# Two transformer blocks on one Trainium2 core: the residual multiplies folded into the norm, and the order of the attention's and mixer's side work changed

## The chip, the core and the metric

The kernel runs on one core of a Trainium2 chip. It is written out engine by engine: TensorE (PE), VectorE (DVE), ScalarE (ACT), GpSimd (POOL) and SyncE (SP) each have an instruction stream in program order, and semaphores join them. The metric is the device time of one execution in microseconds; the figure is the median of several executions.

## The reference

A first block works on 256 tokens of width 1024 (the latents), in fp32: a norm, 8 heads of dilated and 8 heads of block attention with relative bias, cross attention to 256 memory tokens, and a gated feed-forward with a causal convolution. A second part, of two layers, works on 512 tokens: those 256 latents and 256 context tokens (`ctx`), with conditioning vectors.

```python
def rmsnorm(x, g):           # first block
    y = xf * lax.rsqrt(jnp.mean(xf * xf, axis=-1, keepdims=True) + EPS)
    return y * g
    ...
        y = jnp.concatenate([rmsnorm(merge(ya, DIL_WIDTH), g_out_dil[l]),
                             rmsnorm(merge(yb, MOBA_WIDTH), g_out_moba[l])], axis=-1)
        h = h + y @ w_out[l]
        h = h + memory_cross_attention(rmsnorm(h, g_cross[l]), rmsnorm(mem, g_mem[l]), ...)
        h = h + conv_ffn(rmsnorm(h, g_ffn[l]), ...)
...
def modulate(x, shift, scale):
    return x * (1.0 + scale) + shift

def post_norm(x, y):         # second part: behind every mixer and feed-forward
    return layer_norm(ALPHA * x + y)
```

In the second part each of two layers is feed-forward, mixer, feed-forward. Each reads `modulate(x, shift, scale)` of the stream, multiplies its result by a gate, and `post_norm` gives the new stream; ALPHA is 4 to the power 0.25. The shifts, scales and gates come from `silu(c)` by a weight matrix of 1024 to 9 x 1024 a layer ("ada"). The mixer of layer 0 ("even") joins a gated linear attention (GLA, 4 heads, decays that are running sums of log gates, in chunks) with a latent attention (MLA, 4 heads of rope and non-rope parts). The mixer of layer 1 ("odd") is neighbourhood attention with context keys.

## The kernel before

**Tiles and products.** The stream X lies in SBUF as eight tiles X[:, k, :] of 128 features by 512 tokens: columns `lat` hold the 256 latents, columns `con` the 256 context tokens, and before those come in, `con` is scratch (att1's output y). A dense product runs in three passes on fp32r: high parts by high weights (L526), low part of the activation by high weights (L527), high part by low weights (L528). A weight chunk is 8 k-tiles by 256 columns. One DMA on SP's queue brings it into WF (three buffers). ACT casts it to the high part WH in two halves (`act_half`, L1041), DVE subtracts for the low part of the first half (`dve_split`, L1545), POOL for that of the second (`pool_split`, L2174). WH and WL have two buffers each. `PLAN` lists the chunks in the order in which PE uses them, and `splits_at(i)` says which chunk is split while chunk i is used: always the next one. Two chunks that PE interleaves (`pe_pair`) are listed in SECOND. A chunk of 256 columns at 256 tokens is 48 matmuls.

**Engine programs.** `pe_program`, `act_program`, `dve_program` and `pool_program` walk through the same stages, each with the part of its engine. An engine that waits holds up all that stands behind it. PSUM banks are handed out in a ring (`Banks.take`): PE waits for the event that empties the oldest bank.

**Start.** `pe_stat` sums the squares of x; ACT takes the root of the mean (Ln, then Exp); DVE scales a tile, ACT casts its high part and DVE subtracts the low one; then come the chunks qa, ka and va (two each). WIDE[0], the first chunk, is split beside the squares. Between the highs of x's norm and the split of qa's second chunk, ACT does two Silu of c and c_ctx with their table (L1484, L1485) and loads the log table again (L1044). Behind ka, ACT squares the memory and POOL adds the six squares (L2181).

**First attention (att1).** 16 units of one head each go through scores, exp, turning and weighing at steps i, i+2 and i+4 (`pe_attention_pairs`, 19 steps, two units at a time). `work1` lists what else is done in step i: scaling of the memory tiles ("mem"), and the chunks qb, kb, vb (inputs of the last eight heads) and km, vm (memory's keys and values). `work1 = spread(work1, 10) + [[]]*6` puts them all into the steps up to 9. `act_y` and `dve_y` put a finished pair's output into X[:, k, con] and, from k = 4 on, norm the tile four before, over a scratch HT[13]. `pe_pieces` and `dve_pieces` are parts of the ada product for the first gates ("pieces"), and stand behind the y statistic. Then come wout (4 chunks, L1719 adds to X), the cross norm, qm (the first two chunks as a pair), cross attention, wo, and the ffn norm.

**First feed-forward (f0).** `pe_ffn` does 11 gate and up chunks and 8 down chunks a half. The first pair is followed by `pe_ada_turn(5)`, whose bank DVE empties at L1585.

**Transition of the second part.** A feed-forward or mixer ends in `act_collect`, `pe_means` and a norm. `dve_modulate` makes of each X tile a product with the root in TMP[k % 3] (L1783, named "mt"); ACT applies scale and shift (`act_modulate`) and casts, DVE subtracts. While the next stage's chunks run, POOL multiplies each X tile by SQ, which is ALPHA times the root (L2187, `pool_residual`), so that X holds ALPHA times the normed stream, to which `dve_gated` adds gate times product. Into the first feed-forward of the second part (f10) no norm leads: POOL multiplies latents (L2341) and ACT context tiles (in `act_f0`) by ALPHA.

**Mixer of layer 0.** `pe_even`, `act_even`, `dve_even` and `pool_even` walk through e_q, e_lr, e_k, e_c (two chunks), e_v (two), uqn, uqr, e_r (two), ukv, then MLA attention. `gla_items` are the pieces of the GLA (`level` 0 to 19, `gouts`, `gnorms`), taken one by one by `some(n)` at places written out by hand, and the last ones by `work3`, beside the attention. The gates (d, n) in the order (0,0), (1,0), (0,1), (1,1) go through exp, Ln (L1361), a subtraction, and a running sum along the 256 tokens (L2012, two scans each). In the order before, gk is evicted ahead of the Ln, all four gates are scanned behind the split of e_k, and `dve_decays(1)` stands behind the second one.

## Time and profile before

| | us |
|---|---|
| three executions | 2321.92, 2323.25, 2324.7 |
| median | 2323.25 |
| the profiled execution, own time | 2322.09 |
| its span in the profile | 2320.3 |
| busy in the span: PE | 2218.7 (96%) |
| DVE | 1420.0 (61%) |
| ACT | 976.4 (42%) |
| POOL | 755.2 (33%) |
| mean granted clock of PE | 0.985 |

The profiled execution is one of its own; 1.8 us of its time lie outside the span. PE is busy 96% and the other engines far less. Some idle and slow stretches are short and lie at known places, so the views by time tell more than the sums.

### The profile page before, as it was taken

What the parts mean: (1) busy time and instruction counts of PE and PEld (TensorE: products, weight loads), DVE (VectorE), ACT (ScalarE), POOL (GpSimd) and SP (SyncE); (2) the same over time, 40 slices, a digit from 0 to 9 for tenths busy, and PEclk for the clock granted to TensorE, in tenths of its full rate; (3) what the DMA queues carried; (4) which work ended last, traced back from release to release, by engine and by line L of the source; (5) the groups of instructions that cost most, each with busy time, mean ns of one, the idle gap of its engine ahead of it and who ended that gap; (6) DMA issues with size and microseconds to landing.
All of it is one profiled execution on the core that took longest, in us unless ns stands there. A gap on an engine that the chain in (4) does not pass through costs nothing.

```text
span 2320.3 us, 34014 instructions
## 1 busy us (share of the span) xinstructions
PE 2218.7 (96%) x13148; PEld 1906.8 (82%) x13148; DVE 1420.0 (61%) x2103; ACT 976.4 (42%) x1585; POOL 755.2 (33%) x378
## 2 busy tenths in 40 slices
PE   6989989999999998988999999999999999989997
PEld 6978889998888876866788888878888878878997
DVE  3644454548887667757777766579756474447335
ACT  4655446543222336455442222253223254455443
POOL 3424325452222233521233322234222224214543
PEclk9999999999999999999999999999999999999999
DMA  7426535455464331120334443234454362214553
GB/s 256 171 95 263 224 128 191 159 178 198 165 227 168 132 118 51 53 73 1 127 109 150 168 172 119 99 136 152 169 205 158 104 147 92 73 55 140 177 180 105
DMA packets 79406, 329.98 MB, mean 142 GB/s; under 512 B 18912, under 2 KB 29280, under 8 KB 55696
## 3 DMA queue, kind: packets, MB, share of 16 engines
q1 hardware_dynamic: 79248, 327.81, 40.6%
q8 instruction: 107, 1.75, 0.3%
q14 instruction: 51, 0.42, 0.1%
HBM read 326.70 MB, written 1.08 MB: 141 GB/s over the span
## 4 chain that ended last, share of the span: by engine, by line
PE 82%; DVE 7%; issue 5%; ACT 5%; DMA 1%; POOL 0%; DVEq 0%; SPq 0%; ACTq 0%; POOLq 0%
PE ps L526 26%; PE ps L528 25%; PE ps L527 25%; PE ps L711 1%; ACT WH L1041 1%; PE ps L742 1%; DMA WF<-in_w 1%; PE ps L702 1%; DVE TMP L1621 1%; DVE WL L1545 1%; PE ps L687 1%; PE ps L721 1%; DVE AR L1958 0%; DVE TMP L1648 0%; DVE TMP L1560 0%
## 5 line engine op out<-in xcount | busy, mean ns | idle before, releaser
L2174 POOL TENSOR_TENSOR WL<-WF,WH 128x1024 fp32r<-128x1024 f32 (+2 forms) x253 | 598.0, 2364 | 1342.3 <-ACT WH L1041 1341.7
L526 PE MATMUL ps<-Hh,WH 128*128 128x256 f32 (+1 forms) x2536 | 860.3, 339 | 33.9 <-DVE WL L1545 10.8
L527 PE MATMUL ps<-Hl,WH 128*128 128x256 f32 (+1 forms) x2536 | 854.9, 337 | 0.0
L528 PE MATMUL ps<-Hh,WL 128*128 128x256 f32 (+1 forms) x2536 | 854.6, 337 | 0.0
L1041 ACT CAST WH<-WF 128x1024 fp32r<-128x1024 f32 (+3 forms) x507 | 466.3, 957 | 304.8 <-PE ps L528 296.6
L526 PEld LDWEIGHTS ps<-Hh,WH 128*128 128x128 f32 x2536 | 484.8, 191 | 98.9 <-issue 45.6
L528 PEld LDWEIGHTS ps<-Hh,WL 128*128 128x128 f32 x2536 | 484.8, 191 | 49.6
L527 PEld LDWEIGHTS ps<-Hl,WH 128*128 128x128 f32 x2536 | 485.1, 191 | 49.1 <-issue 0.2
L1621 DVE CUSTOM_DVE_ANT_0 TMP<-AR 128x1024 f32<-128x1024 f32 x216 | 416.0, 1965 | 8.6 <-DMA AR<-in_ada 7.3
L1545 DVE TENSOR_TENSOR WL<-WF,WH 128x1024 fp32r<-128x1024 f32 (+2 forms) x254 | 312.8, 1232 | 136.8 <-ACT WH L1041 136.3
L526 PE MATMUL ps<-HIDh,WH 128*128 128x512 f32 (+1 forms) x880 | 307.7, 350 | 3.8 <-DVE WL L1545 3.8
L527 PE MATMUL ps<-HIDl,WH 128*128 128x512 f32 (+1 forms) x880 | 305.7, 347 | 0.0
L528 PE MATMUL ps<-HIDh,WL 128*128 128x512 f32 (+1 forms) x880 | 305.7, 347 | 0.0
L1275 ACT ACTIVATE TMP<-ps 128x512 f32<-128x512 f32 (+1 forms) x88 | 47.8, 543 | 393.4 <-PE ps L528 393.4
L526 PEld LDWEIGHTS ps<-HIDh,WH 128*128 128x128 f32 x880 | 167.3, 190 | 26.6 <-issue 6.3
L527 PEld LDWEIGHTS ps<-HIDl,WH 128*128 128x128 f32 x880 | 167.4, 190 | 21.2 <-issue 0.7
L528 PEld LDWEIGHTS ps<-HIDh,WL 128*128 128x128 f32 x880 | 167.4, 190 | 20.7
L1860 DVE TENSOR_TENSOR TMP<-TMP,ps 128x512 f32<-128x512 f32 (+1 forms) x88 | 54.5, 619 | 184.2 <-PE ps L528 111.6
L1827 DVE SCALAR_TENSOR_TENSOR X<-ps,MOD,X 128x256 f32<-128x256 f32 x136 | 60.3, 479 | 132.9 <-PE ps L528 132.9
L1279 ACT CAST HIDh<-TMP 128x512 fp32r<-128x512 f32 (+1 forms) x88 | 49.9, 567 | 141.5 <-DVE TMP L1860 141.5
L526 PE MATMUL ps<-WH,Hh 128*128 128x256 f32 x320 | 91.9, 287 | 3.5 <-POOL WL L2174 3.5
L1862 DVE TENSOR_TENSOR HIDl<-TMP,HIDh 128x512 fp32r<-128x512 f32 (+1 forms) x88 | 58.6, 666 | 55.7 <-ACT HIDh L1279 55.7
(226 smaller groups left out, 2089.2 us busy)
## 6 DMA issues: line engine op xcount, KB each, us to landing
WF<-in_w SPq DMA_DIRECT2D x170, 1024.0 KB, 4.8
AR<-in_ada SPq DMA_DIRECT2D x120, 512.0 KB, 5.7
WF<-in_w SPq DMA_DIRECT2D x80, 704.0 KB, 4.1
AR<-in_piece SPq DMA_DIRECT2D x12, 1024.0 KB, 8.3
AR<-bias_rows SPq DMA_DIRECT2D x3, 1024.0 KB, 12.8
AR<-in_rpb SPq DMA_DIRECT2D x12, 256.0 KB, 6.6
AR<-in_cond SPq DMA_DIRECT2D x2, 1024.0 KB, 7.6
X<-in_x SPq DMA_DIRECT2D x2, 512.0 KB, 4.6
```

The source lines that it names most:

```text
L526: e.matmul(out, lh, rh, start=first, stop=False, skip_group_check=parts)
L527: e.matmul(out, lh, rl, start=False, stop=False, skip_group_check=parts)
L528: return e.matmul(out, ll, rh, start=False, stop=end, skip_group_check=parts)
L1041: e.copy(h[:, k0:k1, :], src[:, k0:k1, :]).then_inc(*up("w_hi", ("hi", i, q)))
L1275: e.activation(t[:, 0:T], ps[st, "g", n][:, 0:T], ACT.Silu).then_inc(*up("gate", (st, "ga", n)))
L1279: e.copy(HIDh[:, j, 0:T], t[:, 0:T]).then_inc(*up("hid_hi", (st, "hidh", n)))
L1545: e.tensor_tensor(l[:, k0:k1, :], src[:, k0:k1, :], h[:, k0:k1, :].bitcast(F32), ALU.subtract).then_inc(*up("w_lo", ("lo", i, 0)))
L1621: e.tensor_tensor_reduce(out=WIDE_TMP[r], in0=AW[x % 3], in1=COND[:, r, :], scale=1.0, scalar=0.0, op0=ALU.mult, op1=ALU.add, accum_out=MO ...
L1827: e.scalar_tensor_tensor(out=X[:, j, c], in0=ps[tile][:, c], scalar=MOD[:, l, 8 * g + j, r:r + 1], in1=X[:, j, c], op0=ALU.mult, op1=ALU.a ...
L1860: e.tensor_tensor(t, t, ps[st, "u", n][:, 0:T], ALU.mult).then_inc(*up("gated", (st, "m", n)))
L1862: e.tensor_tensor(HIDl[:, j, 0:T], t, HIDh[:, j, 0:T].bitcast(F32), ALU.subtract).then_inc(*up("hid_lo", (st, "hidl", n)))
L2174: e.tensor_tensor(l[:, k0:k1, :], src[:, k0:k1, :], h[:, k0:k1, :].bitcast(F32), ALU.subtract).then_inc(*up("p_lo", ("lo", i, 1)))
```

## The change

The residual multiplies go: gates are made as 1/ALPHA of what they were and the norm's epsilon as EPS/ALPHA^2, which leaves `layer_norm(x + y/ALPHA)` with the same value; DVE writes X times root back into X. In the first part, the order of work changes at the start, in att1, at the cross and ffn norms and in f0; in the mixer of layer 0 the order of Ln, scans, decays, evictions and the group norm changes.

```diff
@@ plan()
-    for c in range(4):
+    for c in range(3):
         out.append(("vm", k8, [("w_kv", rng(1024 + 256 * c, 256))]))
     wide("wout", "w_out", 1024)
+    out.append(("vm", k8, [("w_kv", rng(1024 + 256 * 3, 256))]))
...
-    work1 += [("km", i) for i in range(4)] + [("vm", i) for i in range(4)]
-    work1 = spread(work1, 10) + [[] for _ in range(6)]
+    work1 = [[] for _ in range(19)]
+    for i, items in ((0, [("mem", 0), ("qb", 0)]), (1, [("mem", 1), ("qb", 1)]), (2, [("mem", 2), ("kb", 0)]), (3, [("mem", 3), ("kb", 1)]),
+                     (4, [("vb", 0)]), (5, [("vb", 1)]), (6, [("km", 0)]), (8, [("km", 1)]), (10, [("km", 2)]), (12, [("km", 3)]),
+                     (14, [("vm", 0)]), (16, [("vm", 1)]), (18, [("vm", 2)])):
+        work1[i] = items
...
-    work3 = spread(gla_items[GLA_FIRST:], 16)
+    work3 = [[] for _ in range(19)]
+    for n, item in enumerate(gla_items[GLA_FIRST:]):
+        work3[min(2 * n, n + 6)] = [item]
@@ pe_attention_pairs: the pieces now ahead of the y statistic
-                    pe_stat(e, ("y", end // 4), S, [(HT[10], ("ysum", end // 4)), (HT[11 + end % 2], ("ysq", end))])
                     if end == 7:
                         pe_pieces(e, "y")
+                    pe_stat(e, ("y", end // 4), S, [(HT[10], ("ysum", end // 4)), (HT[11 + end % 2], ("ysq", end))])
@@ pe_ffn
-                pe_ada_turn(e, 5)
...
+                if n == 2:
+                    pe_ada_turn(e, 5)
@@ pe_program: idle matmuls ("load" on zeros, then on X), vm(3) ahead of qm, qm no longer a pair
+        pe_idle(e, "load", 7, zeros[:, 0:P], zeros, ("zeros",))
         pe_stat(e, "x", S, [(HT[0], ("xsum", 7))])
+        pe_idle(e, "x", 5, ident, X[:, 0, lat])
...
-        pe_pair(e, ac, *[(CH["qm"][c], S, [(("qm", j), [("qm", j)]) for j in (2 * c, 2 * c + 1)]) for c in range(2)])
-        for c in range(2, 4):
+        pe_work1(e, "vm", 3)
+        for c in range(4):
@@ act_y, dve_y: the y norm in place, cast and low one step later
-            dve_scaled(e, HT[13], X[:, k - 4, con], vec("g_out", k - 4), STAT[0][:, 0:S], ("yt", k - 4), ("root", ("y", 0)),
-                       ("yl", k - 5) if k > 4 else ("ml", 7))
+            dve_scaled(e, X[:, k - 4, con], X[:, k - 4, con], vec("g_out", k - 4), STAT[0][:, 0:S], ("yt", k - 4), ("root", ("y", 0)))
@@ act_f0, pool_program: gone
-                    e.mul(X[:, n, con], X[:, n, con], ALPHA).then_inc(*up("ctx_x", ("cxx", n)))
...
-            e.tensor_scalar(X[:, k, lat], X[:, k, lat], ALPHA, None, ALU.mult).then_inc(*up("p_x", ("f10", "res", k)))
@@ act_norm of post_norm, dve_modulation
-        e.activation(r, t, ACT.Ln, bias=eps).then_inc(*up("ln", (st, "ln")))
+        e.activation(r, t, ACT.Ln, bias=cst("eps_post")).then_inc(*up("ln", (st, "ln")))
...
-        if g != 3:
-            e.tensor_scalar(m[:, 16:24, :], m[:, 16:24, :], 0.5, None, ALU.mult)
+        e.tensor_scalar(m[:, 16:24, :], m[:, 16:24, :], (1.0 if g == 3 else 0.5) / ALPHA, None, ALU.mult)
@@ dve_modulate
-                    e.tensor_tensor(t[:, 0:T], X[:, k, 0:T], root[:, 0:T], ALU.mult).then_inc(*up("scaled", (st, "mt", k, 0)))
+                    e.tensor_tensor(X[:, k, 0:T], X[:, k, 0:T], root[:, 0:T], ALU.mult).then_inc(*up("scaled", (st, "res", k)))
...
+        e.tensor_tensor(X[:, 0, 0:T], X[:, 0, 0:T], root[:, 0:T], ALU.mult).then_inc(*up("scaled", (st, "res", 0)))
@@ act_even: Ln ahead of the split of e_k's successor and of the gk evictions; QR's con copy and KN
-        for j in range(2):
-            e.wait_ge(*at(("qrrot", j)))
-            e.copy(QR[:, j, con], ps["qr", j][:, con]).then_inc(*up("a_evict", ("qrc", j)))
...
-        for j in (0, 2):
+        for j in range(4):
             act_evict(e, KN[:, j, :], ("kn", j)).then_inc(*up("a_evict", ("kn", j)))
@@ act_program: first chunk's second half no longer ACT's; Silu moved
-        act_split(e, WIDE[0])
+        act_half(e, WIDE[0], 0)
...
-        e.activation(SC[:, :, 0], vec("c", 0, 8), ACT.Silu)
...
+            if c == 0:
+                e.activation(SC[:, :, 0], vec("c", 0, 8), ACT.Silu)
+                e.activation(SC[:, :, 1], vec("c_ctx", 0, 8), ACT.Silu).then_inc(*up("silu", ("silu",)))
+                act_logs(e)
@@ dve_even: scans of (d, 0) behind e_k's split, decays behind e_c's first split, scans of (d, 1) in the loop of e_v
+            if n == 0:
+                scan(d, n)
+        dve_splits(e, CH["e_c"][0])
+        dve_decays(e, 1)
...
         for i in range(2):
             dve_splits(e, CH["e_v"][i])
             some(1)
+            scan(*GATES[2 + i])
...
-        for j in (1, 3):
-            dve_evict(e, KN[:, j, :], ("kn", j))
-        some(2)
+        some(1)
...
+        work = [work3[0], gi + work3[1]] + work3[2:]
+        dve_attention(e, "mla", units3, 192 ** -0.5, work, dve_gla, end)
@@ dve_program: low split of the first chunk's second half; the six adds of the memory squares
+        dve_split(e, WIDE[0], 1)
...
+        for k in range(1, 7):
+            e.tensor_tensor(HT[0], HT[0], HT[k], ALU.add).then_inc(*up("d_sum", ("msum", k)))
@@ pool_program: the high cast of the first chunk's second half
-        pool_split(e, WIDE[0])
+        e.tensor_scalar(parts_of(WIDE[0])[0][:, k0:k1, :], staged(WIDE[0])[:, k0:k1, :], 1.0, None, ALU.mult).then_inc(
+            *up("p_hi", ("hi", WIDE[0], 1)))
...
-        for k in range(1, 7):
-            pool_sum(e, HT[0], HT[k], ("msq", k), ("msum", k - 1) if k > 1 else ("msq", 0), ("msum", k))
```

`pool_residual` goes with all its calls, and so do the SQ product behind `act_modulate` and the waits for it. `splits_at` of the pair (qm 0, qm 1) becomes plain; the chunk split behind wo is still f0_gu[1], and its two high casts now stand behind the squares and behind highs 0 to 2 of the norm.

## Rows read from the trace of the kernel before

**Rows 1.** Page: busy time and instructions of PE in the whole span

```profile
PE 2218.7 (96%) x13148; PEld 1906.8 (82%) x13148; DVE 1420.0 (61%) x2103; ACT 976.4 (42%) x1585; POOL 755.2 (33%) x378
```

**Rows 2.** Windows: PE, PEld, DVE, ACT, POOL busy us (instructions), PE clock, DMA share, GB/s

```profile
25.40:32.65 7.25, 7.16 (x47) 7.19 (x48) 2.68 (x2) 1.80 (x3) 5.52 (x2) 0.76 0.51 164
61.10:153.30 92.20, 91.86 (x793) 89.17 (x794) 49.70 (x111) 52.30 (x111) 39.76 (x17) 1.00 0.44 151
153.30:190.20 36.90, 27.40 (x182) 18.80 (x180) 19.48 (x58) 25.91 (x62) 1.64 (x3) 0.72 0.47 188
302.40:321.20 18.80, 12.19 (x101) 11.81 (x99) 11.12 (x21) 11.35 (x19) 7.78 (x4) 0.97 0.46 154
321.20:335.20 14.00, 14.00 (x96) 14.00 (x97) 5.34 (x8) 3.33 (x6) 2.88 (x2) 0.79 0.26 96
924.10:931.50 7.40, 7.36 (x26) 5.71 (x26) 6.46 (x10) 1.06 (x1) 1.71 (x1) 0.75 0.45 158
```

**Rows 3.** Timeline of the start: start us, us, engine, operation, [idle before <-releaser]

```profile
9.93 1.99 ACT L1041 CAST WH<-WF 128x1024 fp32r<-128x1024 f32 x2 [1.79 <-DMA WF<-in_w]
...
11.00 1.23 DVE L1545 TENSOR_TENSOR WL<-WF,WH 128x1024 fp32r<-128x1024 f32 x1 [1.74 <-ACT WH L1041]
...
11.99 2.44 POOL L2174 TENSOR_TENSOR WL<-WF,WH 128x1024 fp32r<-128x1024 f32 x1 [11.57 <-ACT WH L1041]
...
14.05 1.05 DVE L1560 SCALAR_TENSOR_TENSOR TMP<-X,VEC,STAT 128x256 f32<-128x256 f32 x2 [1.82 <-ACT STAT L1064]
...
15.76 0.55 PE L526 MATMUL ps<-Hh,WH 128*128 128x256 f32 x1 [5.22 <-DVE Hl L1555]
...
23.04 1.99 ACT L1041 CAST WH<-WF 128x1024 fp32r<-128x1024 f32 x2
...
25.49 0.36 PE L526 MATMUL ps<-Hh,WH 128*128 128x256 f32 x1 [1.98 <-DVE WL L1545]
...
26.28 2.40 DVE L1545 TENSOR_TENSOR WL<-WF,WH 128x1024 fp32r<-128x1024 f32 x1 [0.60 <-ACT WH L1041]
```

**Rows 4.** Groups by line, POOL: busy us, mean ns | idle before

```profile
L2187 POOL TENSOR_TENSOR X<-X,SQ 128x512 f32<-128x512 f32 (+1 forms) x40 | 65.2, 1634 | 0.0
...
L2341 POOL TENSOR_SCALAR X<-X 128x256 f32<-128x256 f32 x8 | 7.8, 980 | 1.7 <-DVE Hl L1760 1.7
```

**Rows 5.** Timeline, end of va and first attention's first chunks

```profile
54.79 0.35 PE L526 MATMUL ps<-WH,Hh 128*128 128x256 f32 x1 [1.96 <-POOL WL L2174]
...
58.08 1.99 ACT L1041 CAST WH<-WF 128x1024 fp32r<-128x1024 f32 x2 [6.27 <-DMA WF<-in_w]
```

**Rows 6.** Timeline, tail of the first attention

```profile
161.77 1.55 PE L742 MATMUL ps<-TMP,AR 128*64 128x128 f32 x12
...
167.63 1.55 PE L742 MATMUL ps<-TMP,AR 128*64 128x128 f32 x12
...
183.66 0.88 DVE L1560 SCALAR_TENSOR_TENSOR TMP<-X,VEC,STAT 128x256 f32<-128x256 f32 x2 [3.09 <-ACT STAT L1064]
```

**Rows 7.** Timeline of PE, cross norm

```profile
214.04 0.36 PE L526 MATMUL ps<-Hh,WH 128*128 128x256 f32 x1 [1.67 <-DVE Hl L1555]
```

**Rows 8.** Timeline, first feed-forward

```profile
320.89 0.18 DVE L1585 TENSOR_REDUCE MOD<-ps 128x8 f32<-128x32 f32 x1
...
321.17 0.56 PE L526 MATMUL ps<-Hh,WH 128*128 128x256 f32 x1 [5.03 <-issue]
```

**Rows 9.** Timeline of PE, first chunks behind the mixer of layer 0

```profile
1200.02 0.47 PE L526 MATMUL ps<-Hh,WH 128*128 128x512 f32 x1 [0.73 <-DVE WL L1545]
```

**Rows 10.** Timeline of the mixer of layer 0, e_k to e_c

```profile
918.49 3.37 DVE L2012 TENSOR_TENSOR_SCAN AR<-CST,AR 128x256 f32<-128x256 f32 x2
...
921.78 2.21 DVE L1545 TENSOR_TENSOR WL<-WF,WH 128x1024 fp32r<-128x1024 f32 x1
...
924.14 0.77 PE L526 MATMUL ps<-Hh,WH 128*128 128x512 f32 x1 [7.33 <-DVE WL L1545]
```

**Rows 11.** Timeline of PE, inside the MLA attention

```profile
1099.53 0.68 PE L721 MATMUL ps<-TMP,HAl 128*128 128x128 f32 x4 [3.08 <-issue]
```

More of the change, by code:

```diff
@@ L73, in const_array @@
     put("eps", np.full((P, 1), EPS, np.float32))
+    put("eps_post", np.full((P, 1), EPS / ALPHA ** 2, np.float32))
     put("one", np.ones((P, 1), np.float32))
@@ L1213, in act_collect @@
         after = [(st, "shifted", k) if k < 4 else (st, "x", k)]
-        if k == 0 and st + "res" in RESIDUALS:
-            after.append((st, "res", KT - 1))
         if k in (4, 5, 6):
@@ L1256, in act_modulate @@
                 e.copy(Hh[:, k, 0:T], t[:, 0:T]).then_inc(*up("h_hi", (st + "h", k)))
-        e.mul(SQ[:, 0:T], STAT[0][:, 0:T], ALPHA).then_inc(*up("mean", (before, "up")))
     def act_cond(e, st):
@@ L1355, in act_even @@
             e.activation(TMP[i], TMP[i], ACT.Exp, scale=-1.0).then_inc(*up("decay", ("gexp", d, n)))
+        for i, (d, n) in enumerate(GATES):
+            e.wait_ge(*at(("gexp", d, n)))
+            e.activation(TMP[i], TMP[i], ACT.Ln, bias=one).then_inc(*up("decay", ("gln", d, n)))
         act_splits(e, CH["e_k"][0])
@@ L1358, in act_even @@
             act_evict(e, GK[:, j, :], ("gk", j)).then_inc(*up("a_evict", ("gk", j)))
-        for i, (d, n) in enumerate(GATES):
-            e.wait_ge(*at(("gexp", d, n)))
-            e.activation(TMP[i], TMP[i], ACT.Ln, bias=one).then_inc(*up("decay", ("gln", d, n)))
         for j in range(2):
@@ L2203, in pool_swiglu @@
                 pool_splits(e, CH[st + "_gu"][n])
-                if before and n < KT:
-                    pool_residual(e, st, before, n, T)
             for n in range(KT):
```

159 lines of the change are left out of this document (78 added, 81 removed).

## The prediction, made before the kernel was run

> **What bounds the kernel now.** I read the page's busy times first, then the windows, then the timeline around each hole of the matmul engine. PE is busy 2218.7 us of a span of 2320.3 us [rows 1], so it is the bound, and only two things can be won without removing matmuls: the 101.6 us in which it idles, and the stretches in which its matmuls run at half pace after an idle. The chain of waits says the same, since nearly all of it lies on matmul lines. The windows show where both sit [rows 2]. From 61.1 to 153.3 us, where each pair of attention steps has weight chunks beside it, PE is busy 91.86 of 92.2 us at a granted clock of 1.00. From 153.3 to 190.2, where the chunks have run out, it is busy 27.40 of 36.9 at a mean of 0.72, so more than half of the time at the lower of its two levels (1.2 and 2.4 GHz). The same pattern, smaller, stands at 302.4 to 335.2 and at 924.1 to 931.5. The change adds idle matmuls and moves the rest, so I price it as idle time removed, plus pace won back, minus holes that appear.
>
> **Start.** PE's first product comes at 15.76, and its next hole ends at 25.49, where it waits for a low split [rows 3]. That split waits for ACT's high casts at 23.04, which stand behind the two Silu instructions and their two table loads. The change moves Silu and both tables into the first key chunk, which has slack. So the 1.98 us wait goes, and with it the slow stretch behind it: 25.4 to 32.65 has 7.16 us of matmul at a mean clock of 0.76 [rows 2], which at full clock is 7.16 x 0.76 = 5.4, so 1.7 less. Against it stands the cast of the second half of the first chunk, now on POOL, and its low split, now on DVE ahead of the norm. No row shows POOL casting such a tile. Its subtract of the same tile took 2.44 us [rows 3]; its own tensor_scalar on 256 columns took 0.98 [rows 4], so four of them are 3.9, which is the upper end, and DVE's pace on the tile, 1.23, is the lower. I take 2.4, the row of the same shape. From 9.9, when the tile is there and ACT casts it now, it ends at about 12.4. DVE's first split runs beside it; a DVE subtract beside a POOL one took 2.40, alone 1.23 [rows 3], so it ends at 13.4 and the second at 14.6, and the norm, which could begin at 14.05, begins some 0.7 later (0 to 2.2). Start: -2.0 -1.7 +0.7 = -3.0, range -1.5 to -4.5. The seven and five idle matmuls fill time in which PE waits anyhow (5.22 us before 15.76), cost nothing, and may bring the first chunk to full clock (a rival, below).
> That the two subtracts met is what the trace shows, and it speaks against a POOL cast in this place. The Trainium skill, SBUF — State Buffer, section "SBUF: two separate sides", goes further: a DVE operation with two SBUF inputs and a GpSimd operation share a port pair under an exclusive lock, and the first to start holds it for its whole instruction. By that rule DVE's split would start only behind the cast, at 12.4, and both end near 14.9, the norm 0.8 late. The page GPSIMD Engine Reference, section "Engine selection", says that one-input operations on GpSimd run at roughly line rate; by that the cast would be done near 11.2 and the norm not late at all, so the start would be -3.7. No row here shows a POOL cast of this size.
> The six adds of the memory norm move from POOL to DVE. The wait of 1.96 us at 54.79 for POOL's low split, which stood behind them, goes [rows 5], but the cast at 58.08 waited 6.27 us for its transfer, and that one isn't earlier by more than PE's slack behind it. I count -0.7, range 0 to -1.9.
>
> **First attention.** The items of work1 stood at steps 0 to 9; now they reach step 18, so the last pairs get a chunk each. In the old tail a pair of steps came every 5.86 us (161.77, 167.63) [rows 6] with little matmul in it. What PE did in 153.3 to 190.2 is 27.40 x 0.72 = 19.7 us of work at full clock [rows 2]. One value chunk (vm 3) leaves the stage: 48 matmuls of 0.12 us, 5.8. So 13.9 of work stands there, and the idle that can't be filled: the chain from the last statistic to the first scaled tile (the norm's first tile comes at 183.66, 3.09 after DVE's last work [rows 6]), 3.2 by itself. 13.9 + 3.2 = 17.1 against 36.9 would be -19.8. I take -18, since seven chunks can't fit ten gaps evenly, range -12 to -21. The y norm now done in place adds no instruction, only an order: high casts shift one step later, behind ACT evictions that have slack at 52.3 busy of 92.2 [rows 2].
> The chunk vm 3 comes back in front of the query chunks, beside the cross norm. There PE waited 1.67 us for the norm [rows 7]; of the 5.8 the hole swallows that: +4.1, range +3.5 to +5. The feed-forward norm's casts, moved: -0.3 (0 to -0.6).
>
> **First feed-forward.** PE is busy 12.19 of 18.8 us from 302.4 to 321.2, and 14.00 of 14.00 at 0.79 behind it [rows 2]. The hole of 5.03 us ends when DVE has reduced the bank of the ada turn (320.89, then the matmul at 321.17) [rows 8]. With the turn behind chunk 2 no chunk waits for that bank. Idle 6.6 + pace 14.0 x 0.21 = 2.9 makes 9.5; what stays is ACT's pace of casts, for which I leave three small holes of 2.6 in sum. So -6.8 (range -4 to -8.5). What is late next: ACT's high cast of the fourth chunk. The eight X*ALPHA of ACT and of POOL (0.98 us each [rows 4]) go; nobody waited for them.
>
> **The residual pass.** POOL's multiply by ALPHA times the root, 40 of them, 65.2 us [rows 4], has idle POOL around it, so removing it is worth nothing by itself. DVE now writes X times root into X where it wrote a temporary: same count, and one multiply more per transition, 0.7 us behind the low parts, under a chunk pair of some 22 us. What the pass did cost is the port: DVE slows beside POOL, and at the transition behind the mixer PE waited 0.73 for DVE's low split at 1200.02, which follows DVE products that ran beside POOL's multiplies [rows 9]. Four such transitions: -1.0, range 0 to -3. The factor ALPHA moves into the gates and the root's epsilon: nothing.
>
> **Mixer of layer 0.** The hole before 924.14 is 7.33 us, behind DVE: two scans (3.37), decays, then the low split of 2.21 [rows 10]. The next 7.4 us run at 0.75 [rows 2], so 1.8 more. Now the second pair of scans stands beside the value chunks, Ln of the gates ahead of ACT's evictions of gk, and the split of the first c chunk before the decays. So both go, and 0.2 of small ones: -9.3 (range -5 to -9.5). The scans then delay the c norm beside e_v by about 1.0; the level item moved off ACT's copies gives about 1.0 back. The KN evictions, all four on ACT now, and the group norm taken into attention step 1 lift part of the holes around the MLA attention (3.08 us at 1099.53 [rows 11]): -2, range 0 to -3. Mixer: -11.3.
>
> **Sum.** -3.0 -0.7 -18 +4.1 -0.3 -6.8 -1.0 -11.3 = -37.0. The profiled execution took 2322.1 us (span 2320.3 and 1.8 around it), 1.2 under the median of 2323.25; 2322.1 - 37.0 = 2285.1, and I say 2285.
>
> **Rivals.**
> 1. *The attention pairs are set by DVE and ACT, not by PE.* If a pair needs its old 5.86 us and the chunk beside it isn't overlapped (11.6 a pair against 8.56), six and a half pairs cost 20 us more: 2305. (8.56 is a chunk of 5.8 and a pair's matmuls, 2.8.) Against it: 91.86 of 92.2 us busy with DVE at 49.7 and ACT at 52.3 [rows 2]. Chance 0.12.
> 2. *Slower: the stage falls to the lower clock.* Where the chunks are spread thinly over steps 6 to 18, a hole per pair may keep PE at 1.2 GHz. The rows show it: the old tail ran at 0.72 with its holes, and the stretch behind the hole of 5.03 us at 0.79 [rows 2, 8]. The stage has some 58 us of PE work at full clock from step 6 on (seven chunks of 5.8, 13.9 of the tail, 4 of the pairs ahead); at half clock that is 58 more, so 2285 + 58 = 2343, slower by 21. It decides from 37 us of such work on, where the gain is used up; it needs in every pair a hole like the one at 25.49, behind which the clock fell. A chance of 0.04, since the one long stretch with chunks has 0.34 us of idle in all. The Trainium skill, TensorE: Matmul & The Clock Gate, "HAM oscillation", says that micro-idles of PE can make the clock swing between its levels; by that rule such a stage would be slow throughout.
> 3. *More is won.* The idle matmuls warm the first chunk (worth what it was worth behind 25.49, 1.7), the holes before the mixer's scores and in the first feed-forward close wholly, and the att1 tail reaches 19.8: 2285 - 9 = 2276. Chance 0.15.
> 4. *Holes only move.* The feed-forward waits one chunk later (+4), the mixer waits in the c norm (+5) as the scans are now ahead of it: 2294. Chance 0.10.
> 5. *The change doesn't do what it says:* the tail stays, since the spread chunks wait for their splits and PE idles ahead of them for as long as before: 2285 + 18 = 2303, and 2320 if the first feed-forward and the mixer keep their holes too (6.8 + 11.3). Chance 0.02.
>
> **How the numbers follow.** The forecast, 2285, has chance 0.57 with a range of its own of 2277 to 2293. The whole range runs from rival 3's lower side, 2272, to most of rival 1, 2302; it leaves out rivals 2 and 5 and the upper side of 1. About 0.2% of this kernel, 4.6 us, is what a measurement can tell from no change. Slower is rival 2 (0.04), same 0.02 for rival 5's far end and what lies between, the rest faster.
>
> **What the profile after should show.** Start: first product between 16 and 17, no hole near 25, clock 1.00 from then on. Att1: 153 to the first wout chunk at 1.00 with PE over 90% busy; y's norm at some 165 to 172. A value chunk ahead of the query chunks. F0: no hole over 2 us. Mixer: no hole over 2 us between the k and v chunks; DVE's second scans beside L526 of e_v. No POOL rows of L2187. POOL's busy time down by 65 to 80 us. PE idle falls from 101.6 to some 78: of the 37.0, 1.7 + 7.7 + 2.9 + 1.8 = 14.1 is pace and not idle. Wrong would be: clock under 0.9 in att1, or a PE wait for a scan or a c norm over 4 us.

## The result, and the profile after

The changed kernel takes 2297.09 us (median of 2292.81, 2294.47, 2299.71 and 2299.92) against 2323.47 beside it: a ratio of 0.9885, interval 0.9865 to 0.9905. That is 26.4 us less; the forecast was 38 less and 2285, and 2297 lies in the range of 2272 to 2302. The profiled execution is the one of 2299.92, the slowest of the four; its stages say more than its sum.

The page of the changed kernel: span, busy times, and the chain that ended last by engine.

```profile
span 2298.1 us, 33979 instructions
...
PE 2221.8 (97%) x13172; PEld 1911.5 (83%) x13172; DVE 1404.5 (61%) x2117; ACT 970.0 (42%) x1571; POOL 677.7 (29%) x324
...
PE 86%; DVE 6%; ACT 4%; issue 3%; DMA 1%; POOL 1%; DVEq 0%; SPq 0%; ACTq 0%; POOLq 0%
```

POOL's busy time fell by 77.5 us and the span by 22.2. PE is idle 76.3 us instead of 101.6, where some 78 was foretold. PE's busy time rose by 3.1 us, with the idle matmuls in it (1.2 to 6.8 us and 10.3 to 13.8, some 9 us), so the others lost about 6 of it; 14.1 of pace were to be won back. The holes that remain have slow stretches behind them too.

The account by stages is made from PE's first product of each stage, in the two profiled executions.

| stage | before | after | difference | foretold |
|---|---|---|---|---|
| start to the first chunk of att1 | 60.99 | 57.64 | -3.35 | -3.7 |
| att1, to wout | 123.15 | 108.12 | -15.03 | -18 |
| wout, vm 3, qm, to wo | 74.57 | 79.94 | +5.37 | +4.1 |
| cross attention's output, ffn norm, to f0 | 31.91 | 31.26 | -0.65 | -0.3 |
| f0 | 231.94 | 224.29 | -7.65 | -6.8 |
| f10 | 348.18 | 349.55 | +1.37 | 0 |
| mixer of layer 0 | 284.75 | 284.74 | -0.01 | -11.3 |
| all behind it, to the end of the span | 1164.80 | 1162.59 | -2.21 | -1.0 |
| sum | 2320.29 | 2298.13 | -22.16 | -37.0 |

The row of the mixer is the answer to most of the question: a price of 11.3 us was given, and the stage is as long as before. The changed kernel's 284.74 us are at the long end, though. Three edited kernels below with the very same mixer (f1_turn_old, s1_no_idle, s3_rows_late) take 282.5 us in their profiles, a fourth (a1_work1_old) 283.8; so the fair difference is about -2.2 us, still far from -11.3.

Windows of the changed kernel over the stages of [rows 2]: att1 in two parts, the first feed-forward's start, and the e_c chunks of the mixer.

```profile
57.60:124.60 67.00, 66.77 (x567) 63.96 (x567) 44.73 (x106) 40.89 (x95) 25.84 (x12) 0.95 0.42 146
124.60:165.70 41.10, 37.24 (x312) 32.72 (x309) 20.84 (x51) 27.91 (x65) 12.47 (x7) 0.96 0.55 198
276.90:307.00 30.10, 29.24 (x236) 28.54 (x237) 19.88 (x37) 17.42 (x28) 10.25 (x5) 1.00 0.37 121
896.60:904.00 7.40, 7.40 (x45) 5.94 (x44) 4.64 (x4) 3.03 (x4) 4.17 (x2) 1.00 0.20 53
```

The bare tail of att1 is gone: 37.24 of 41.1 us busy at 0.96, where [rows 2] had 27.40 of 36.9 at 0.72. The feed-forward has 0.86 us of idle in 30.1. From 896.6 to 904.0, where the hole of 7.33 us had ended, PE is busy all the time at full clock.

Timeline of the start: start, duration, engine, operation, idle time before it and its releaser.

```profile
9.64 2.77 POOL L2312 TENSOR_SCALAR WH<-WF 128x1024 fp32r<-128x1024 f32 x1 [9.21 <-DMA WF<-in_w]
...
10.66 1.23 DVE L1560 TENSOR_TENSOR WL<-WF,WH 128x1024 fp32r<-128x1024 f32 x1 [1.47 <-ACT WH L1048]
...
12.44 1.23 DVE L1560 TENSOR_TENSOR WL<-WF,WH 128x1024 fp32r<-128x1024 f32 x1 [0.56 <-POOL WH L2312]
...
15.10 0.36 PE L529 MATMUL ps<-Hh,WH 128*128 128x256 f32 x1 [1.35 <-DVE Hl L1570]
...
55.19 1.99 ACT L1048 CAST WH<-WF 128x1024 fp32r<-128x1024 f32 x2 [8.56 <-DMA WF<-in_w]
...
57.64 0.55 PE L529 MATMUL ps<-Hh,WH 128*128 128x256 f32 x1 [3.58 <-DVE WL L1560]
```

The first product comes at 15.10, not between 16 and 17. POOL's cast took 2.77 us, beyond my 2.4, and yet the norm starts at 13.58, ahead of the old 14.05 [rows 3]: ACT, free of the second cast, has the root 1.25 us earlier (12.77 against 14.02). The norm could have begun then, but stands behind DVE's second low split, which waits for POOL's cast. The last two rows show that from there on PE's gain is lent: the cast of the next chunk waits 8.56 us for its transfer (6.27 before [rows 5]), PE waits 3.58 us behind it, and a slow stretch follows.

Five waits of PE in att1, wout and the mixer of the changed kernel (1.65 and 1.5 us at 1022.00, 1003.24 and 1073.54 are of the same order as the smaller ones).

```profile
138.14 0.96 PE L705 MATMUL ps<-AR 64*128 64x128 f32 x12 [2.58 <-DVE TMP L1653]
...
169.25 0.36 PE L529 MATMUL ps<-Hh,WH 128*128 128x256 f32 x1 [1.00 <-DVE Hl L1570]
...
934.11 1.16 PE L877 MATMUL ps<-AR 64*128 64x128 f32 x15 [1.42 <-POOL AR L2251]
...
966.96 1.35 PE L885 MATMUL ps<-AR 64*128 64x256 f32 x10 [3.03 <-DVE AR L1953]
...
1015.14 1.05 PE L877 MATMUL ps<-AR 64*128 64x128 f32 x14 [2.87 <-POOL AR L2251]
```

None of the five was in the forecast by place. The fourth and fifth are inside the mixer and are what the runs below take apart.

### The profile page after: what moved, and what is told of

Read it like the earlier page. It is cut to its first block, busy times and chain, and to the rows that moved or that the text cites. A ratio compares the mean times of both kernels' runs of the same rounds, so it can differ in the third digit from the quotient of the medians.

```text
span 2298.1 us, 33979 instructions
## 1 busy us (share of the span) xinstructions
PE 2221.8 (97%) x13172; PEld 1911.5 (83%) x13172; DVE 1404.5 (61%) x2117; ACT 970.0 (42%) x1571; POOL 677.7 (29%) x324
## 3 DMA queue, kind: packets, MB, share of 16 engines
q8 instruction: 107, 1.75, 0.3%
## 4 chain that ended last, share of the span: by engine, by line
PE 86%; DVE 6%; ACT 4%; issue 3%; DMA 1%; POOL 1%; DVEq 0%; SPq 0%; ACTq 0%; POOLq 0%
PE ps L529 27%; PE ps L531 26%; PE ps L530 26%; DMA WF<-in_w 1%; PE ps L714 1%; PE ps L705 1%; ACT WH L1048 1%; PE ps L745 1%; PE ps L690 1%; PE ps L724 0%; DVE WL L1560 0%; POOL WL L2204 0%; DVE AR L1972 0%; PE ps L676 0%; DVE TMP L1663 0%
## 5 line engine op out<-in xcount | busy, mean ns | idle before, releaser
L2204 POOL TENSOR_TENSOR WL<-WF,WH 128x1024 fp32r<-128x1024 f32 (+2 forms) x252 | 588.5, 2336 | 1412.5 <-ACT WH L1048 1412.1
L1636 DVE CUSTOM_DVE_ANT_0 TMP<-AR 128x1024 f32<-128x1024 f32 x216 | 399.6, 1889 | 9.9 <-DMA AR<-in_ada 9.0
L1560 DVE TENSOR_TENSOR WL<-WF,WH 128x1024 fp32r<-128x1024 f32 (+1 forms) x255 | 313.8, 1230 | 123.1 <-ACT WH L1048 122.0
## 6 DMA issues: line engine op xcount, KB each, us to landing
AR<-bias_rows SPq DMA_DIRECT2D x3, 1024.0 KB, 13.8
```

The lines of the kernel that those rows point to most:

```text
L1560: e.tensor_tensor(l[:, k0:k1, :], src[:, k0:k1, :], h[:, k0:k1, :].bitcast(F32), ALU.subtract).then_inc(*up("w_lo", ("lo", i, q)))
L1636: e.tensor_tensor_reduce(out=WIDE_TMP[r], in0=AW[x % 3], in1=COND[:, r, :], scale=1.0, scalar=0.0, op0=ALU.mult, op1=ALU.add, accum_out=MO ...
L2204: e.tensor_tensor(l[:, k0:k1, :], src[:, k0:k1, :], h[:, k0:k1, :].bitcast(F32), ALU.subtract).then_inc(*up("p_lo", ("lo", i, 1)))
```

## The experiments

All runs are of the changed kernel with one part edited, unless it says otherwise. A ratio is to the kernel before, on the same chip; for the changed kernel it is 0.9885 (0.9865 to 0.9905). Each interval reaches some 4.5 us to either side, so between two edited kernels a difference of a few us in the medians says little (only m5_w3_qr's 9 us is near the edge of what they resolve), and what follows is read from stages of the profiles. Each kernel has one profile.

### The mixer as a whole: old order (m1_mixer_old)

```diff
-            if n == 0:
-                scan(d, n)
-        dve_splits(e, CH["e_c"][0])
-        dve_decays(e, 1)
+            scan(d, n)
+            if i == 1:
+                dve_decays(e, 1)
...
-            scan(*GATES[2 + i])
```

> The changed kernel with the whole mixer of layer 0 in its old order (Ln, scans, decays, rotation copy, evictions, group norm, places of the level items). Theory A (the mixer's part of the change is worth nothing, since moved items give back what the closed hole wins): 2297 us, within 2 us of the changed kernel; the hole of 7 us before e_c's second half is back, and the mixer takes its old 283.2 us from the first product of e_q to the last one. Theory B (the mixer won its 11 us, and something outside it, the clock or DMA, lost as much): 2308 us.

The other edits of the mixer are undone with it, as in the diffs further down. Median 2295.23, ratio 0.9871 (0.9854 to 0.9888): not slower than the changed kernel. Theory A is right in its main point: the reordering of the mixer is worth nothing. But it expected the hole of 7 us back, and that was wrong. DVE's last scans and PE's wait ahead of e_c's second chunk:

```profile
893.02 1.27 DVE L2025 TENSOR_TENSOR_SCAN AR<-CST,AR 128x256 f32<-128x256 f32 x2
...
895.56 0.76 PE L527 MATMUL ps<-Hh,WH 128*128 128x512 f32 x1 [3.11 <-DVE WL L1561]
```

The wait is 3.11 us and not 7.33, and the mixer takes 282.51 us, though every order in it is old. Something else in the change had shortened it already.

### The residual pass alone (r1_no_residual)

The kernel before, with the multiplies taken out, X times root written in place, and no order changed (excerpt):

```diff
@@ pool_swiglu, pool_even, pool_odd
-                if before and n < KT:
-                    pool_residual(e, st, before, n, T)
@@ dve_modulation
+        e.tensor_scalar(m[:, 16:24, :], m[:, 16:24, :], (1.0 if g == 3 else 0.5) / ALPHA, None, ALU.mult)
@@ dve_modulate
+                    e.tensor_tensor(X[:, k, 0:T], X[:, k, 0:T], root[:, 0:T], ALU.mult).then_inc(*up("scaled", (st, "res", k)))
```

> The kernel before with the residual multiplies alone taken out (gates over ALPHA, epsilon over ALPHA squared, X times root in place), all orders old. Theory A (the multiplies held the port that DVE needs for the scans of the mixer, so their removal alone shortens the hole before e_c's second half from 7.5 us to 3 or 4, and gives 1 us at each later transition): mixer of layer 0 in 278 to 280 us instead of 284.75, time 6 to 9 us under the kernel before. Theory B (as predicted: POOL's work was covered, only 1 us is won at the transitions): 0 to 2 us under the kernel before, the hole stays above 7.

Median 2318.51 over ten executions, ratio 0.9975 (0.9965 to 0.9985), so 3.5 to 8 us less, where I had foretold 1.0 for the whole pass. Theory A holds for the hole (7.33 to 3.12 us), not for its total of 6 to 9 us; the mixer takes 282.56 us, 2.2 less and not 5 or 6, since another stage gives back (below). DVE's last scans, its low split and PE's wait in this kernel:

```profile
918.68 1.27 DVE L2009 TENSOR_TENSOR_SCAN AR<-CST,AR 128x256 f32<-128x256 f32 x2
...
919.87 1.20 DVE L1543 TENSOR_TENSOR WL<-WF,WH 128x1024 fp32r<-128x1024 f32 x1
...
921.21 0.77 PE L526 MATMUL ps<-Hh,WH 128*128 128x512 f32 x1 [3.12 <-DVE WL L1543]
```

The same two instructions took 3.37 and 2.21 us before [rows 10]. What ran beside them on POOL before was first its own low split, then a residual multiply, the timeline of the kernel before says:

```profile
921.27 1.64 POOL L2187 TENSOR_TENSOR X<-X,SQ 128x512 f32<-128x512 f32 x1
```

It ends at 922.91, and DVE's split of 2.21 us, begun at 921.78, ends 1.1 us behind that, which is about what the split takes alone (1.20). The scan, on the other hand, was not beside a residual multiply but beside POOL's low split (918.73 to 921.31), which it meets only because DVE is 1.1 us late, and that comes from an earlier residual multiply. In the timeline of the kernel before, a DVE subtract that takes 0.41 us in the kernel without the multiplies:

```profile
912.44 1.48 POOL L2187 TENSOR_TENSOR X<-X,SQ 128x512 f32<-128x512 f32 x1
...
912.69 1.51 DVE L1918 TENSOR_TENSOR AR<-AR 128x256 f32<-128x256 f32 x1
```

So 1.1 for this subtract, 2.1 for the scan and 1.0 for the split make the 4.2 us by which the hole shrank. In a groups-by-line view, the scans before (busy, mean ns):

```profile
L2012 DVE TENSOR_TENSOR_SCAN AR<-CST,AR 128x256 f32<-128x256 f32 x8 | 8.3, 1077 | 0.1
```

and without the residual pass:

```profile
L2009 DVE TENSOR_TENSOR_SCAN AR<-CST,AR 128x256 f32<-128x256 f32 x8 | 6.2, 815 | 0.1
```

Eight scans of the same size, 1077 ns against 815; all of the difference is the one scan of 2.76 us, which takes 0.66 without the multiplies. A second scan takes 1.75 us in both kernels, beside a POOL product of 1.28.

What was given back lies between uqr's first product and the second half of e_r's first chunk, 14.03 us before and 16.21 here. The kernel before, then this one, DVE's instruction being the same subtract of the GLA:

```profile
981.63 4.49 POOL L2174 TENSOR_TENSOR WL<-WF,WH 128x1024 fp32r<-128x1024 f32 x1
...
981.78 0.43 DVE L1924 TENSOR_TENSOR AR<-AR 128x256 f32<-128x256 f32 x1
```

```profile
978.62 2.47 POOL L2171 TENSOR_TENSOR WL<-WF,WH 128x1024 fp32r<-128x1024 f32 x1
...
978.77 2.61 DVE L1921 TENSOR_TENSOR AR<-AR 128x256 f32<-128x256 f32 x1
```

The two begin 0.15 us apart in both kernels. Before, POOL was the one held up (4.49 us instead of 2.47), which nobody waited for; here it is DVE (2.61 instead of 0.43), and the stage is longer by the same 2.18 us. All six edited kernels with the old order in this place have it too (16.2 us). What decides which of the two is held isn't in the profile, so that the kernel before was spared these 2.2 us in its profile was luck.

### The scans alone (m4_scans_only)

Rotation copy, evictions, group norm and level items as before, scans, Ln and decays new (the edit is that of m1_mixer_old without its lines on scans).

> The changed kernel with only the scans, Ln and decays of the mixer in the new order; rotation copy, evictions, group norm and level items as before. Theory A (the scans alone win 9.3 us and cost 1.2 at the latent norm, and all else in the mixer's part costs): 2289 to 2291. Theory B (the other items pay by themselves): 2299 or more, as the KN hole of 3 us and the 3.3 us hole at the end of the attention come back.

Median 2291.49, ratio 0.9864 (0.984 to 0.9887). The mixer takes 280.45 us, 2.1 less than with everything old (m1). From the second half of e_c's first chunk to e_v's first product: 18.96 us against 23.90, 4.9 less. But each of the two has one stretch of 3.4 us at half clock on the way from e_q to e_v: m1 behind its hole, m4 ahead of this count, behind the products of the gates (the second half of e_k takes 8.08 us against 6.47). From e_q's first product to e_v's it is 59.31 against 62.66, so the scans' order wins 3.3: the hole of 3.11 us is gone, the stretch only stands elsewhere. From e_v's first product to the second half of e_v's last chunk: 25.16 against 24.00, the 1.2 that the scans cost beside the value chunks (foretold 1.0).

### The level items of the MLA attention (m2_work3_old)

```diff
-    work3 = [[] for _ in range(19)]
-    for n, item in enumerate(gla_items[GLA_FIRST:]):
-        work3[min(2 * n, n + 6)] = [item]
+    work3 = spread(gla_items[GLA_FIRST:], 16)
```

> The changed kernel with the last GLA items at their old attention steps (1, 3, 5, ... instead of 0, 2, 4, ...). Theory A (in the MLA attention PE now stands in a level item ahead of the turning, waiting for an exp that ACT does only behind the roots): the attention from its first scores to the first output product takes 70 to 72 us instead of 74.4, and the time is 2292 to 2295. Theory B (the attention is longer because of the group norm on DVE in step 1, or the slow clock): attention unchanged at 74 us, time 2297.

Median 2291.65, ratio 0.9859 (0.9841 to 0.9876); the mixer takes 280.75 us. From the value products (mv) to the output chunks: 78.38 us against 81.51. The chain is in ACT's timeline of the changed kernel. ACT loads tables and takes the roots of the group norm, and only then does the exp for which POOL, and behind it PE (1015.14 above), wait:

```profile
1007.27 1.28 ACT L1303 ACT_TABLE_LOAD   x1
...
1012.19 1.04 ACT L1338 ACTIVATE AR<-AR 128x1024 f32<-128x1024 f32 x1
```

At step 2 PE meets this item ahead of the turning of the first head. DVE's division for that turning stands behind DVE's own part of the item (it starts at 1016.63), so both wait for ACT's exp. That is theory A, but the waits are only part of the price: PE idles 12.68 us in the stage in the changed kernel and 11.81 in this one, and 16.3 against 11.5 us of it are at half clock. So 0.9 us is waiting and the larger part is pace. In the six profiles with the new steps the stage takes 81.1 to 81.5 us, in this one and the three kernels built on it 77.5 to 78.4. The output chunks behind it give 1.0 back (54.98 us with the new steps, 56.00 here), which leaves a price of 1.75 us for the mixer.

### The rotation copy and the split of uqr (m3_qr_old)

```diff
+        for j in range(2):
+            e.wait_ge(*at(("qrrot", j)))
+            e.copy(QR[:, j, con], ps["qr", j][:, con]).then_inc(*up("a_evict", ("qrc", j)))
@@ dve_even
+        some(1)
         dve_splits(e, CH["uqr"][0])
-        some(1)
...
-            e.tensor_copy(QR[:, j, con], ps["qr", j][:, con]).then_inc(*up("d_evict", ("qrc", j)))
```

> The changed kernel with the copy of the rotary context columns back on ACT, and DVE's split of uqr back behind the level item. Theory A (these two put DVE 2 to 3 us late: holes of 1.0 us and 3.2 us at the level items between uqn and e_r): those holes are again 0.3 and 1.1, the slow stretch behind them is gone, and the time is 2292 to 2294. Theory B (DVE is late there because the scans now stand beside the value chunks): holes unchanged, 2297.

Median 2295.3, ratio 0.9874 (0.9858 to 0.9891). From uqr's first product to the second half of e_r's first chunk: 16.20 us against 17.63 (17.18 in the five other profiles with this order, which lack its slow stretch). So it costs 1.0 to 1.4 us, and theory A's size was too large, and its time of 2292 to 2294 was missed: of the wait of 3.03 us (966.96), 2.12 stay, now for POOL instead of DVE, which is the place shown under r1_no_residual.

### Both put back (m5_w3_qr)

> The changed kernel with the level items of the attention and the rotation copy and split of uqr in the old places, and scans, evictions and group norm new. Theory A (the two costs are at different places and add up): mixer of layer 0 in 278 to 280 us, time 5 to 6 us under the changed kernel. Theory B (they share one chain, so only the larger counts): mixer 280.5 to 281, 4 us under.

Median 2287.96 (2287.11 to 2291.34), ratio 0.9846 (0.9826 to 0.9866): the fastest kernel of the study, 9 us under the changed one by the medians, more than the stage shows: the mixer takes 279.74 us. Against the 282.5 us of the other profiles with the mixer as changed the fair difference is 2.8; m2 alone has 1.75 and m3 alone 0.4 against the same 282.5. The costs add up (2.15 to 2.8): theory A for the mixer, while its 5 to 6 us in time was too little.

### DVE's group norm later (b2_norm_step6)

In m5_w3_qr the largest wait of the attention stands behind DVE's group norm in step 1 (timeline of DVE and PE in m5_w3_qr):

```profile
1006.68 1.40 DVE L1980 SCALAR_TENSOR_TENSOR TMP<-TMP,VEC,STAT 128x512 f32<-128x512 f32 x1
...
1008.67 0.68 DVE L1985 TENSOR_TENSOR AR<-TMP,AR 128x512 f32<-128x512 f32 x1
...
1011.33 1.01 PE L875 MATMUL ps<-AR 64*128 64x128 f32 x6 [3.53 <-DVE AR L1973]
```

and about it lies the longest slow stretch of the whole kernel, which begins at 1007.7, before the wait does (a window of m5_w3_qr; PE clock is the last column but two):

```profile
1007.70:1018.00 10.30, 6.34 (x31) 4.77 (x30) 9.53 (x21) 2.79 (x7) 1.27 (x1) 0.50 0.01 2
```

```diff
-        work = [work3[0], gi + work3[1]] + work3[2:]
+        work = work3[:6] + [work3[6] + gi] + work3[7:]
```

> m5_w3_qr with DVE's first group norm (3.3 us of multiplies) in attention step 6, behind the level items of steps 1, 3 and 5, instead of in step 1. Theory A (in step 1 it makes DVE late for the level item, and PE waits 3.6 us there): that hole falls under 1.5 us, the attention from its first evicted value product to the output chunks takes 2 to 4 us less than the 77.9 of m5_w3_qr, and the time is 2284 to 2286. Theory B (the hole waits for ACT's roots, which stand ahead of its exp for the same item): the hole stays above 2.5 us, 2288.

Median 2289.79, ratio 0.986 (0.9842 to 0.9879): no gain, where 2284 to 2286 was expected. PE's waits:

```profile
1011.66 0.58 PE L875 MATMUL ps<-AR 64*128 64x128 f32 x2 [0.94 <-DVE AR L1973]
...
1033.69 0.41 PE L712 MATMUL ps<-CST,TMP 128*128 128x128 f32 x2 [1.50 <-DVE TMP L1664]
```

The wait fell from 3.53 to 0.94 us as theory A says, and a wait of 1.50 us appeared at 1033.69, where the norm stands now. The attention takes 77.52 us from its value products on, against 77.87. A hole that was filled in one step came back in another, since DVE has the same work.

### The order of att1 (a1_work1_old)

```diff
+    work1 = [("qb", 0), ("qb", 1), ("kb", 0), ("kb", 1), ("vb", 0), ("vb", 1)]
...
+    work1 += [("km", i) for i in range(4)] + [("vm", i) for i in range(3)]
+    work1 = spread(work1, 10) + [[] for _ in range(6)]
```

> The changed kernel with the chunks of work1 at their old steps (all up to step 9), vm 3 still behind wout. Theory A (the spread of the chunks wins all of the attention's part, since the last six steps are bare otherwise): from the first chunk of the attention to wout 117 us (the old 123.15 less the chunk that left, 5.8) instead of 105 to 108, time 2306 to 2309, and the lower clock back in the last 35 us of the stage. Theory B (the in-place norm and the ada pieces ahead of the statistic win part of it): 110 to 113 us, 2300 to 2303.

Median 2304.68, ratio 0.9915 (0.9894 to 0.9935). From the first chunk to wout 118.04 us. Theory A: the difference to before, 5.1, is about the chunk that moved out (5.8), and nearly everything else comes from the spread; its time of 2306 to 2309 was 1.3 us too high at its lower end. Windows of it, the chunks' part and the tail:

```profile
57.40:140.00 82.60, 81.01 (x688) 78.26 (x689) 46.51 (x109) 48.14 (x105) 35.72 (x15) 0.98 0.45 157
140.00:175.50 35.50, 25.34 (x190) 18.13 (x189) 15.39 (x47) 21.16 (x55) 4.47 (x4) 0.81 0.29 116
```

The old tail is back, 25.34 of 35.5 us at 0.81. In the eleven profiles that have the new att1, the stage takes 104.7 to 110.1 us.

### The ada turn of f0 (f1_turn_old)

```diff
+                pe_ada_turn(e, 5)
...
-                if n == 2:
-                    pe_ada_turn(e, 5)
```

> The changed kernel with the ada turn of the first feed-forward back behind the first pair. Theory A (chunk 2 or 3 waits for the turn's bank): the hole of 5 us is back, the first feed-forward takes 231 us again instead of 224.3, the time is 6 to 8 us above the changed kernel's. Theory B (the hole moved for another reason, a cast that came earlier): 0 to 2 us.

Median 2302.77, ratio 0.9909 (0.9889 to 0.993). The time is 5.7 us above the changed kernel's by the medians (6 to 8 expected). f0 takes 231.80 us against 224.29: the step is worth 7.5, and the hole of [rows 8] is back to the hundredth:

```profile
303.14 0.55 PE L529 MATMUL ps<-Hh,WH 128*128 128x256 f32 x1 [5.03 <-issue]
```

### The start (s1_no_idle, s3_rows_late, b1_m5_rows)

Without the 12 idle matmuls:

> The changed kernel without the 7 and 5 idle matmuls at the start. Theory A (they alone bring qa's chunks to full clock 4 us earlier, but what they win is lost while PE waits for the transfer of the first qb chunk): the first product comes no earlier, qa to the end of va takes 3 to 4 us more, the hole at the first attention chunk shrinks by as much, and the time is the same within 2 us. Theory B (the start is bound by PE): 2 to 4 us slower than the changed kernel.

Median 2295.92, ratio 0.9876 (0.9859 to 0.9893). va's last product starts at 53.08 instead of 52.05, not 3 to 4 us later, and the wait ahead of the first att1 chunk shrinks from 3.58 us to 1.71:

```profile
56.80 0.36 PE L529 MATMUL ps<-Hh,WH 128*128 128x256 f32 x1 [1.71 <-DVE WL L1558]
```

The chunk itself starts at 56.80, earlier than in the changed kernel's profile. Even that 1 us isn't shown to be theirs: in the eleven profiles that have the idle matmuls va's last product starts between 51.42 and 53.59, since the first chunk meets a slow stretch in some of them and not in others. What they may win, nobody can use. With the bias tables' transfers one place later on SP:

```diff
-            if i == 6:
+            if i == 7:
                 sp_rows(e)
```

> The changed kernel with the three bias-table transfers issued on SP behind the first attention chunk's transfer instead of ahead of it. Theory A (that chunk's cast waits 8.6 us because its transfer runs beside the tables'): the hole of 3.6 us before it and the slow stretch behind it go, the first attention chunk starts 2 to 4 us earlier, time 2292 to 2295. Theory B (the softmax then waits for the tables, or the buffers come free too late for an earlier transfer): the hole moves to the first turning, 2297 or more.

> Both: the old places of the attention's level items and of the rotation copy and split (as in m5_w3_qr, 2288.0), with the bias tables' transfers behind the first attention chunk's. If the two are independent: 2284 to 2286, under all kernels so far. If the table transfers only move the hole: 2288.

Medians 2294.44 (0.9869, 0.985 to 0.9888) and 2291.27 (0.9855, 0.9835 to 0.9875; m5_w3_qr alone: 2287.96). In s3_rows_late the first chunk starts at 53.75, 3.9 us earlier, but the second one waits:

```profile
60.70 1.99 ACT L1048 CAST WH<-WF 128x1024 fp32r<-128x1024 f32 x2 [1.32 <-DMA WF<-in_w]
...
63.15 0.36 PE L529 MATMUL ps<-Hh,WH 128*128 128x256 f32 x1 [3.39 <-DVE WL L1560]
```

The wait of 3.39 us stands one chunk later (in the changed kernel, those two chunks run through). In sum the first 60 us are bound by what SP's queue brings, and theory B, that the hole moves, holds in its form if not in its place: it moved to the next chunk and not to the turning. wout is reached at 163.89, within the 161.17 to 165.76 of the kernels without this edit. The time of s3 lies in theory A's range all the same, so here the time alone would have misled; and b1, expected at 2284 to 2286 or at 2288, is 3 us above even the second.

## Why the prediction was right, and where it was not

**Att1 and vm 3.** Right in mechanism, 3 us too large in this profile. The spread is worth 10 to 13 us beyond the chunk's 5.8 (118.04 against 104.7 to 108.3 in all profiles but s3's), so other profiles of the same order reach the -18. The idle of 3.2 us that I left for the norm was too little: a wait of 2.58 us for DVE at 138.14, and 1.00 at wout, came with a slow stretch. vm 3 cost 5.4 and not 4.1: the cross norm's hole of 1.67 [rows 7] closed as foretold, but the wait of 1.00 at wout is new (5.8 - 1.67 + 1.00 = 5.1).

**The start.** The sum was right (-3.7; -3.35), two of its terms were not, and that they cancelled is luck. The norm was put 0.7 late and came 0.5 early. The sum left out that ACT, with one cast less, has the root 1.25 us earlier; against that root the norm is 0.8 late, for DVE's second low split. And a DVE subtract of 1.23 us lay wholly beside POOL's cast (10.66 to 11.89 in 9.64 to 12.41) and wasn't lengthened. That speaks against carrying over the row of two subtracts (2.40 [rows 3]) to a cast, and against the rule of the Trainium skill, SBUF — State Buffer, "SBUF: two separate sides", as I used it there: by it DVE should have waited. In all twelve profiles with this cast the two durations are the same; whether the cast was the one lengthened isn't shown, since none ran alone. And PE gained twice as much up to the end of va (7.0 us), of which half went into the wait for a transfer. That transfer I had named as what bounds the gain.

**The first feed-forward.** -6.8 foretold, -7.65 in the profile, 7.5 by taking it back. The step was right; its parts were off and cancelled. In the first 45 us of f0, where all of the difference lies, idle time fell by 5.7 us (6.62 to 0.89; 4.0 foretold, since I had left 2.6 for small holes), and pace gave 1.9 (2.9 foretold).

**The residual pass.** The step that failed first: "removing it is worth nothing by itself", with 1.0 us for the port. It is worth some 5 us (3.5 to 8). I had the port among the costs, but only at the transitions; the rows of the mixer's scans and split (3.37 and 2.21 [rows 10]) were on the page in front of me, and I took them as DVE's plain prices, though the low split stands at 1.23 in [rows 3]. Here the Trainium skill's rule (same section: a GpSimd operation that reads SBUF and a DVE operation with two SBUF inputs exclude each other) fits the trace: 2.76 us against 0.66 for a scan that met POOL's low split, 2.21 against 1.20 for a split that met a residual multiply. Of the 4.2 us won at that hole, 2.2 were given back at e_r, where DVE and POOL met the other way round. The stages behind the mixer took 2.2 us less (1162.64 against 1164.80), against the 1.0 foretold for the transitions.

**The mixer.** The step that failed in size: -11.3, against 0 in the two profiles and -2.2 by the fair figure, and those 2.2 are what the residual pass alone gives (r1_no_residual, 282.56). The orders, for which the 11.3 were booked, are worth nothing: m1_mixer_old, where all are old, has 282.51. Taken one at a time:

| put in | mixer from | to | difference |
|---|---|---|---|
| scans, Ln and decays (m1 to m4) | 282.51 | 280.45 | -2.1 |
| KN evictions on ACT, group norm in step 1 (m4 to m5) | 280.45 | 279.74 | -0.7 |
| rotation copy and split of uqr (m5 to m2) | 279.74 | 280.75 | +1.0 |
| level items at new steps (m2 to f1, s1, s3) | 280.75 | 282.5 | +1.7 |

Two errors made it. The hole of 7.33 us plus its slow stretch was booked whole to the scans' order; 4.2 of it went with the residual pass, so the order had 3.1 of waiting left to win, won 3.3 up to e_v (m4 against m1) and lost 1.2 beside e_v. And the items that I priced at nothing or as gains were costs: the level items' new steps 1.7 (3.1 in the attention, of which 1.0 comes back behind it), the rotation copy and split of uqr on DVE 1.0. The KN evictions and the group norm win 0.7 and not 2. That the sum is nothing to a tenth is chance, for slow stretches alone move a stage by 1 to 2 us. In the profile, the hole of 7.33 us was closed on the spot, as foretold (-9.3 from the second half of e_c's first chunk to e_v), and given back within 170 us: 1.2 at e_v, 3.6 between uqr and e_r (2.2 of it the chance meeting of DVE and POOL), 1.2 up to the value products, 3.0 in the attention and 0.3 behind it.

**The rivals.** Rival 4, that holes only move, is nearest to what happened, and its 2294 is near the 2297 measured; it had a chance of 0.10. But it put the moved holes in the feed-forward, where none came, and in the c norm, and its price for the mixer was 5 where about 9 were missing. The pairs were not bound by DVE and ACT as rival 1 has it, and the slow clock (rival 2) came only in single stretches (0.95 and 0.96 in the two windows of att1). Rival 3's warm start came true in this profile and in five more of the eleven with the idle matmuls, and was worth nothing.

**What stays open.** Kernels whose first stages are the same reach wout up to 4.6 us apart (161.17 and 165.76), and the four executions of the changed kernel by 7. The stretches at half clock stand at other places in each profile (one of 3.4 us at 500.7 in the changed kernel accounts for f10's +1.37). That a hole is followed by one in some executions and not in others is shown (a wait of 2.82 us leads into f10 in all fourteen profiles, and only six have a slow stretch there); why isn't, and no run tested it. The wait at 138.14 wasn't tried either.

## What to carry to other kernels

A hole's price belongs to everything that makes its last instruction late: look at the durations of the instructions in front of it, and where the same form is faster elsewhere in the trace, ask what ran beside it before booking the hole to the order of work. Each item that is moved into a place where nobody waits makes its engine later for the next one; an order written by hand is best tested item by item, since here two of the moves and one side effect gave back all that the others won. Removing multiplies from POOL, which is 33% busy, that nobody waited for was worth some 5 us, because DVE instructions that PE waited for had been lengthened beside it. And before a stage's difference is explained, look at other kernels with the same code in it: one profile against one was 2 us off here.

## What the runs showed of the hardware

- A POOL tensor_scalar cast of 128x1024 took 2.77 us with a DVE two-input subtract of 1.22 or 1.23 us wholly inside it, unlengthened, in twelve profiles; of two two-input operations, POOL's and DVE's, that overlapped, one was lengthened (DVE's split 2.21 and 2.40 us instead of 1.20 to 1.23, a scan 2.76 instead of 0.66).
- Which of the two is lengthened can change with nothing in the program's order there: a DVE subtract and a POOL subtract that began 0.15 us apart took 0.43 and 4.49 us in the kernel before, 2.61 and 2.47 in r1_no_residual.
- Idle matmuls ahead of the first chunk gave no gain clear of scatter: va's last product starts at 53.08 without them, between 51.42 and 53.59 with them.
- In the MLA attention of m5_w3_qr, PE was granted 0.50 for 10.2 us from 1007.7 on, behind a wait of 1.54 us and with one of 3.53 in it. Shortening the second to 0.94 did not end it: in b2_norm_step6 there are 6.8 us at the low level from 1010.3 on, and 3.4 more behind the new wait of 1.50.
